# One down projection of a two-layer block: five of its eleven k-tile pairs by Strassen's 7-product form

## The reference, cut to what matters

```python
# first layer, x: (256, 1024)
x = x + (g_a * y_a + g_b * y_b) @ w_out           # mixer
h = rms_norm(x, ffn_norm_w)
gt, up = split(h @ w_gate_up, 2)                  # 2 x 2816 columns
x = x + (silu(gt) * up) @ w_down                  # w_down: (2816, 1024)   <- here
# second layer
h = rms_norm(x, norm1_g_2)
proj = h @ w_in_2                                 # next: x2, q, k, g2, v
...
x = x + square(relu(rms_norm(x, norm2_g_2) @ w_up_2)) @ w_down_2   # last projection
```

## Time and profile before

| | us |
|---|---|
| median of three runs | 717.55 |
| profiled execution, its own time | 717.69 |
| its span, first to last instruction | 716.0 |
| PE busy in the span | 710.5 |
| DVE busy | 535.0 |
| ACT busy | 424.2 |
| POOL busy | 190.6 |
| first down projection, first matmul to the first of `x2` | 378.89 to 440.11 |
| last down projection | about 630 to 712.7 |

### The profile page before, as it was taken

The page is one execution under the profiler, slowest core; times in us unless marked ns, Lnnn a source line. Parts: engine busy times, 40 slices in busy tenths (PEclk is TensorE's granted clock), DMA queues, the critical chain, the costliest instruction groups (busy, mean ns, idle before and its releaser), DMA issues.

```text
span 716.0 us, 9290 instructions
## 1 busy us (share of the span) xinstructions
PE 710.5 (99%) x3488; PEld 591.1 (83%) x3488; DVE 535.0 (75%) x715; ACT 424.2 (59%) x550; POOL 190.6 (27%) x128
## 2 busy tenths in 40 slices
PE   9999999999999999999999999999999999999998
PEld 7777878888888888888888888888889888888886
DVE  6899999999987665555556454678866577879997
ACT  7646676664893554444444255469845777865660
POOL 1298998989300030000000000144000134000000
PEclk9999999999999999999999999999999999999999
DMA  9877446455557556555665555633354565655541
GB/s 318 265 221 236 132 162 206 156 170 176 177 192 249 161 184 211 180 176 178 186 210 168 185 194 170 231 138 120 119 174 143 183 206 158 199 181 205 199 177 59
DMA packets 79739, 131.59 MB, mean 184 GB/s; under 512 B 4064, under 2 KB 37032, under 8 KB 79696
## 3 DMA queue, kind: packets, MB, share of 16 engines
q1 hardware_dynamic: 79008, 130.28, 55.0%
q10 hardware_dynamic: 544, 0.53, 0.2%
q0 software_dynamic: 144, 0.20, 0.1%
HBM read 129.75 MB, written 1.25 MB: 183 GB/s over the span
## 4 chain that ended last, share of the span: by engine, by line
PE 96%; DVE 1%; POOL 1%; DMA 1%; ACT 1%; issue 1%; SPq 0%; ACTq 0%
PE acc L1950 21%; PE acc L1952 21%; PE acc L1951 21%; PE aux L1906 4%; PE aux L1610 3%; PE acc L1906 3%; PE acc L1961 3%; PE acc L1962 3%; PE acc L1963 3%; PE aux L1912 2%; PE acc L1912 2%; PE aux L1962 1%; PE aux L1961 1%; PE aux L1963 1%; PE aux L1653 1%; PE aux L1671 1%
## 5 line engine op out<-in xcount | busy, mean ns | idle before, releaser
L1099 DVE TENSOR_TENSOR w_lo<-raw,w_hi 128x2048 fp32r<-128x2048 f32 (+1 forms) x96 | 215.2, 2246 | 86.3 <-ACT w_hi L745 86.3
L745 ACT ACTIVATE w_hi<-raw 128x2048 fp32r<-128x2048 f32 (+2 forms) x115 | 214.6, 1870 | 85.6 <-PE acc L1952 69.6
L1950 PE MATMUL acc<-w_hi,h_both 128*128 128x512 f32 x488 | 195.0, 400 | 0.4 <-DVE tok L1191 0.4
L1952 PE MATMUL acc<-w_hi,h_both 128*128 128x512 f32 x488 | 190.6, 391 | 0.0
L1951 PE MATMUL acc<-w_lo,h_both 128*128 128x512 f32 x488 | 190.1, 390 | 0.0
L1950 PEld LDWEIGHTS acc<-w_hi,h_both 128*128 128x128 f32 x488 | 91.7, 188 | 20.2 <-issue 1.4
L1952 PEld LDWEIGHTS acc<-w_hi,h_both 128*128 128x128 f32 x488 | 91.6, 188 | 19.7
L1951 PEld LDWEIGHTS acc<-w_lo,h_both 128*128 128x128 f32 x488 | 91.8, 188 | 17.7
L606 POOL TENSOR_TENSOR w_lo<-raw,w_hi 128x2048 fp32r<-128x2048 f32 x21 | 97.9, 4677 | 1.4 <-ACT w_hi L745 1.4
L1180 DVE SCALAR_TENSOR_TENSOR aux<-glu_t,vec_t,aux 128x256 f32<-128x256 f32 x232 | 93.6, 485 | 0.0
L629 POOL TENSOR_TENSOR rstd<-ms,nhalf 128x2 f32<-128x2 f32 x3 | 8.0, 2682 | 267.4 <-DVE ms L1161 256.5
(11 more groups left out here) (295 smaller groups left out, 1115.4 us busy)
## 6 DMA issues: line engine op xcount, KB each, us to landing
raw<-w_in_dram SPq DMA_DIRECT2D x29, 1024.0 KB, 5.2
raw<-w_down_dram SPq DMA_DIRECT2D x26, 1024.0 KB, 4.9
raw<-w_gate_up_dram SPq DMA_DIRECT2D x44, 512.0 KB, 4.8
raw<-w_up_dram SPq DMA_DIRECT2D x16, 1024.0 KB, 5.5
raw<-w_out_dram SPq DMA_DIRECT2D x8, 1024.0 KB, 5.1
raw<-w_in_dram SPq DMA_DIRECT2D x12, 512.0 KB, 4.7
raw<-w_proj_attn_dram SPq DMA_DIRECT2D x4, 1024.0 KB, 5.0
raw<-w_proj_conv_dram SPq DMA_DIRECT2D x4, 1024.0 KB, 5.0
```

The costliest lines, as they stand in the source:

```text
L745: ins = nc.scalar.activation(hi_cell(u)[:, part, :], src, ACT.Copy)
L1099: ins = nc.vector.tensor_tensor(lo_cell(u)[:, part, :], src, f(hi_cell(u)[:, part, :]), ALU.subtract)
L1950: nc.tensor.matmul(o, x_h, w_hi[:, slot, j, :], start=begin_, stop=False)
L1952: mm = nc.tensor.matmul(o, x_l, w_hi[:, slot, j, :], start=False, stop=end_)
```

## The change

The first down projection gets the same form as the last one.

- All 1024 columns are computed at once, pair of k-tiles by pair, in the order 0, 1, 2, 6, 3, 4, 7, 5, 8, 9, 10. Pairs 1 to 5 are fast (a `raw` and a `sum` unit), the other six are plain. That is 16 steps (62 to 77) in the place of 12, so B is 78 instead of 74.
- POOL makes the stationary sums of pairs 1 to 5 during the feed-forward stage. ACT first copies the turned tile to `ff_kept`, and later makes `m_hi` and `a_hi_f` from it; DVE makes `m_lo` and `a_lo_f`.
- DVE makes the weight sums of each fast pair (at step `s` those of unit `s + 4`).
- A fourth cell (`w_hi_3`, `w_lo_3`, where `h_both` lies) is used in this stage too, from step 64 to 75.
- The first pair (step 62) is multiplied for the right columns first; then PE waits for the last product of the feed-forward part (`ff_made` 22) and multiplies it for the left columns. Before the first fast product (step 63) PE claims all four `aux` banks, bank 0 with `ff_lo` 11, the last feed-forward pair read by DVE.
- DVE combines the seven products at step B-3 (step 75), the small chain moves from step 62 to step B-2 (76), and the left half is added to `x_res` at step B-1 (77).
- PE multiplies the last two pairs (steps 76, 77) by halves: both left halves, the right half of pair 9, then it waits for `added` 6, turns the left half of `x_res`, and multiplies the right half of pair 10.

```diff
+FAST_1, FAST_2 = range(1, 6), range(2, 10)
+GROUPS_1 = [0, 1, 2, 6, 3, 4, 7, 5, 8, 9, 10]
-    out += [("res", 2 + i, w["w_down"], CW * i, None, list(range(0, FK, UK)), FK) for i in range(2)]
+    out += [("res", 3, w["w_down"], 0, None, list(range(len(block_plan(GROUPS_1, FAST_1)))), KT * FK)]
...
+    for u in range(ALL):
+        wide = u in plan and u not in (D1, D1 + 1, B - 2, B - 1, NU, NU + 1, NU + 2)
+        cells = [k for k in range(SPLIT + 1) if k < SPLIT or wide]
+        if SPLIT in cells and users.get(SPLIT, 0) < (D1 if u < NU else NU):
+            users[SPLIT] = (D1 if u < NU else NU) - 1
+        cell = min(cells, key=lambda k: users.get(k, k - SPLIT))
+        cell_before.append(users.get(cell, -1))
...
@@ POOL
+                for i in FAST_1:
+                    if s == end["ff", i]:
+                        pool.wait_ge(ff_copied, FAST_1.index(i) + 1)
+                        stationary_sums(FAST_1.index(i), ff_kept[:, :].rearrange("p (a b) -> p a b", a=1),
+                                        a_sum[:, 0:1, :, :])
@@ ACT
-                    if s == end["ff", i] + 1:
+                    if s == end["ff", i] + 1 and i not in FAST_1:
                         pair_high(m_hi, i, i % 2, ff_turned, i + 1, ff_hi)
+                    if s == end["ff", i] + 1 and i in FAST_1:
...
+                        nc.scalar.activation(ff_kept[:, :], aux[:, i % 2, :], ACT.Copy).then_inc(ff_copied, 1)
...
+                if s == B - 1:
+                    square_of(2, 0)
+                    square_of(2, 1)
+                    stage_high(2, 0)
+                    stage_high(2, 1)
@@ DVE
+                if s < NU and s + LEAD + 2 in SUMS:
+                    weight_sums(s + LEAD + 2)
...
+                if s == B - 3:
+                    combine(True, None, None, (v_sum_1, w_sum_1, p_kept_1))
+                if s == B - 1:
+                    dve.wait_ge(combined, COMBINED)
+                    dve.wait_ge(last_block, 1)
+                    for t in range(NT):
+                        xr = x_res[:, t, 0:CW]
+                        nc.vector.tensor_tensor(xr, block_acc(s, 0, t), xr, ALU.add).then_inc(added, 1)
+                    stage_low(2, 0)
+                    stage_low(2, 1)
-                if s == begin["res", 2]:
+                if s == B - 2:
                     steps = [0]
@@ PE
+            def last_pairs():
+                for u in (B - 2, B - 1):
+                    wait_blocks(u)
+                tile_pair(B - 2, 0, False, False)
+                tile_pair(B - 1, 0, False, True).then_inc(last_block, 1)
+                tile_pair(B - 2, 1, False, False).then_inc(unit_done, 1)
+                pe.wait_ge(added, 6)
+                stage(2, (0, 1))
+                tile_pair(B - 1, 1, False, True).then_inc(unit_done, 1)
+            def blocks_unit(u):
+                kind, g = plan[u]
+                wait_blocks(u)
+                if u == D1:
+                    tile_pair(u, 1, True, False)
+                    pe.wait_ge(ff_made, 2 * FF // 256)
+                    mm = tile_pair(u, 0, True, False)
...
+                if kind == "raw":
+                    if is_first:
+                        if u < NU:
+                            claim(range(4), combined, COMBINED)
...
+                    product(aux[:, 0, :], u, 0, *of_m(2 * g, 0), is_first, is_last)
+                    product(block_acc(u, 0, 0), u, 1, *of_sum(u, g, 2), False, False)
+                    mm = product(block_acc(u, 1, 0), u, 2, *of_m(2 * g + 1, 0), False, False)
+                if kind == "sum":
+                    product(aux[:, 1, :], u, 0, *of_sum(u, g, 0), is_first, is_last)
+                    product(aux[:, 3, :], u, 1, *of_m(2 * g, 1), is_first, is_last)
+                    product(aux[:, 2, :], u, 2, *of_sum(u, g, 1), is_first, is_last)
+                    mm = product(block_acc(u, 1, 1), u, 3, *of_m(2 * g + 1, 1), False, False)
```

More of the change, by code:

```diff
@@ L55, with block_plan @@
 VROWS = 64
+FAST_1, FAST_2 = range(1, 6), range(2, 10)
+GROUPS_1 = [0, 1, 2, 6, 3, 4, 7, 5, 8, 9, 10]
+GROUPS_2 = [0, 1, 10, 2, 3, 11, 4, 5, 12, 6, 7, 13, 8, 9, 14, 15]
+def block_plan(groups, fast):
+    out = []
+    for g in groups:
+        out += [("raw", g), ("sum", g)] if g in fast else [("plain", g)]
+    return out
 def weight_chunks(w):
@@ L107, in build @@
     FAST_UPS = range(1, 5)
[L108 to L115, removed]
+    D1, B = begin["res", 3], begin["x2", 0]
+    plan = {D1 + p: x for p, x in enumerate(block_plan(GROUPS_1, FAST_1))}
+    plan |= {NU + p: x for p, x in enumerate(block_plan(GROUPS_2, FAST_2))}
+    ALL = max(plan) + 1
+    SUMS = [u for u in plan if plan[u][0] == "sum"]
+    LAST_FAST = {u < NU: u for u in SUMS}
+    raw_no, raw_user = [], []
+    for u in range(ALL):
+        if u not in SUMS:
+            raw_user.append(u)
+        raw_no.append(len(raw_user) - 1)
+    cell_of, cell_before, users = [], [], {}
+    for u in range(ALL):
+        wide = u in plan and u not in (D1, D1 + 1, B - 2, B - 1, NU, NU + 1, NU + 2)
[4 more added lines that the diff above has]
+        cell_before.append(users.get(cell, -1))
+        cell_of.append(cell)
+        users[cell] = u
+    LAST_WIDE = max(u for u in range(B) if cell_of[u] == SPLIT)
     PIECED = 3
@@ L120, in build @@
     raw_value = []
[L121 to L127, removed]
+    for r, u in enumerate(raw_user):
+        paired = u < NU and chunks[units[u][0]][4] is not None
+        raw_value.append((raw_value[r - RAW] if r >= RAW else 0) + (0 if u < PIECED else 32 if paired else 16))
     def on_pool(u):
@@ L558, in _ @@
                             sp.dma_start(tile[ps, :, ps], src).then_inc(lru_w_in, 16)
[L559 to L571, removed]
+            for u in range(NU, ALL):
+                if u not in SUMS:
+                    slot_free(u)
+                    pair_of_tiles(u, a["w_down_2"])
             o_rows = out.rearrange("b (t p) d -> p (b t) d", p=P)
@@ L1874, in after, with product, of_m @@
                     suffixes(3)
+            def product(o, u, j, a_h, a_l, begin_, end_):
+                w_h, w_l = hi_cell(u)[:, j, :], lo_cell(u)[:, j, :]
+                nc.tensor.matmul(o, a_h, w_h, start=begin_, stop=False, skip_group_check=True)
+                nc.tensor.matmul(o, a_h, w_l, start=False, stop=False, skip_group_check=True)
+                return nc.tensor.matmul(o, a_l, w_h, start=False, stop=end_, skip_group_check=True)
+            def of_m(kt, t):
+                return m_hi[:, kt, P * t:P * (t + 1)], m_lo[:, kt, P * t:P * (t + 1)]
@@ new lines, in tile_pair @@
+            def tile_pair(u, n, begin_, end_):
+                g = plan[u][1]
+                for k in range(2):
+                    for t in range(NT):
+                        mm = product(block_acc(u, n, t), u, 2 * k + n, *of_m(2 * g + k, t), begin_ and k == 0,
+                                     end_ and k == 1)
+                return mm
+            def last_pairs():
[7 more added lines that the diff above has]
+                tile_pair(B - 1, 1, False, True).then_inc(unit_done, 1)
@@ L1889, in _ @@
                     pe.wait_ge(*freed_by(c - 2))
+                if is_first and chunks[c][:2] == ("x2", 0):
+                    pe.wait_ge(added, 6)
+                if s in plan:
+                    if s == B - 1:
+                        last_pairs()
+                    elif s != B - 2:
+                        blocks_unit(s)
+                        after(s)
+                    continue
                 if is_first and chunks[c][:2] == ("up", 1):
```

359 lines of the change are left out of this document (205 added, 154 removed).

## The result

The changed kernel takes 721.97 us (median of four runs, 721.83 to 722.04) beside 717.8 us for the kernel before (717.4 to 718.11): 4.2 us slower, ratio 1.0058, 95% interval 1.0041 to 1.0076. The forecast was slower by 2.35 us, 719.9, with a range from 717.9 to 721.9.

A forecast was written before the change was run, and what follows sets the result against it. The prediction took PE's matmuls to bound the stage. Its terms, -3.4 + 1.7 + 0.65 + 3.4 = +2.35 us, on 717.55 us gave 719.9 us, with a range of 717.9 to 721.9 us.

The forecast's parts named there:

- PE's saving: First down projection: 249 matmuls in place of 264, 15 fewer at 0.227 us each, saving 3.4 us.
- The handover of bank 0: Step 62 to 63: PE must wait for DVE's low part of the last feed-forward pair, losing 1.7 us.
- The chain from unit 74 to the additions: Steps 74 to 78: DVE's list takes 17.0 us, PE asks after 13.6 us, so PE waits 3.4 us.
- POOL and ACT in the feed-forward stage: Feed-forward stage: the added sums and copies cost nothing, 0, at most 1 us.
- The end, from B on: From B on, each engine finds its list as before and the last down projection is unchanged: 0.
- The remark that moving the chain alone would leave a wait of 2 us in ACT's list: Step 77 on: without the small chain, ACT's late squares and copies would make PE wait 2 us.
- The term of 0.65 us for DVE's lag: Steps 63 to 75: PE waits briefly for DVE's low parts, 0.65 us, between 0 and 3.
- A rule that would add to this: Gap at B-1: an idle array falls back to 1.2 GHz; noted, but nothing added to the sum.
- rival 1: Behind the gap at B-1 the clock falls, adding 2.7 to 5.4 us: 722.6 to 725.3 us, chance 0.06.
- the prediction's own two signs of being wrong: Wait before the transposes under 1.5 us, or PE's clock below 1.00 anywhere behind it.
- Rivals 2 and 3: First: DVE bounds the whole stage, 721.4 to 723 us, chance 0.08. Second: DVE's list in time, 715.9 us, chance 0.09.
- Rival 3: Whole stage: DVE's list is in time, so only matmuls and handover count: 715.9 us, chance 0.09.

The follow-up runs named there:

- e2_chain: Changed kernel with only the chain of 15 small DVE operations moved from step B-2 to step B+1: 720.92 us.
- e4_bank: Changed kernel with only the last feed-forward pair turned into aux bank 2 in place of bank 0: 721.33 us.
- e6_lists_bank: e3_lists with only the last feed-forward pair put in aux bank 2, pairs in the old order: 716.81 us.
- e1_fill: Changed kernel with twelve unused matmuls of 512 columns put before PE's wait for the additions to x_res: 720.25 us.
- e3_lists: Changed kernel, small chain at B+1; at B-1 ACT squares and stages before copying unit 79, DVE adds to x_res before unit 78's low part: 717.22 us.
- e5_best: e3_lists with the last feed-forward pair in bank 2 and both middle plain pairs behind the second fast pair: 715.14 us.
- e8_lists_chain: e3_lists with the chain of 15 small operations back at step B-2, in front of the additions: 718.47 us.
- e10_fill6: Changed kernel with six unused matmuls in PE's gap at B-1, in place of the twelve of e1_fill: 720.29 us.

## Why the prediction was wrong

The direction, the place and the largest wait were right; the size was short by 1.8 us of 4.2, and the time lies 0.07 us outside the range. The fall of the clock is 1.7 us of this. Beside that the forecast started from 717.55 us, and the kernel before took 717.8 beside the changed one: by the change of 4.2 us alone, 721.7, the time would lie just inside the range.

**What held.** PE's saving, at the spacing of starts and not at the busy time of a row. The handover of bank 0 (1.7 forecast, 1.9 measured: DVE's low part ends at 386.45 us, and PE starts 0.31 us behind it, where 0.06 was reckoned). The chain from unit 74 to the additions: 17.0 us forecast; from 422.17, PE's first start behind unit 74, to 438.85 it took 16.7. PE asked after 13.6 us, as forecast, so the wait was 3.1 us and not 3.4. POOL and ACT in the feed-forward stage: 0, and POOL's sums took 0.46 us each, not 2.67. The end, from B on: 0. The remark that moving the chain alone would leave a wait of 2 us in ACT's list: 2.1 (e2_chain).

**What came out by luck.** The term of 0.65 us for DVE's lag. It was to be waits for DVE's low parts at pair 6 and pair 7. The trace has none of them: PE starts unit 67 at 396.60 us without a wait. That DVE is close behind is shown by e4_bank and e6_lists_bank, where PE comes earlier and waits until about 396.1 us for the low part of this unit. The 0.7 us measured are starts 0.2323 in place of 0.2267 us apart, a mechanism that the prediction doesn't have.

**What failed.** The sum, at the step "A rule that would add to this": it set the clock's price at 0 and left the fall to rival 1 at 0.06. The price was 1.7 us: the last 12 matmuls took 4.4 us in place of 2.7. A clock below 1.00 behind the wait was also one of the prediction's own two signs of being wrong. The fall came in all four runs (granted clock 0.997 or 0.998 of the whole kernel beside 0.999 or 1.0). The argument was that no row of before shows a fall, and that the gap is a single one; but before has no gap of this length (the longest wait of PE that its trace shows is 1.1 us), so its rows could say nothing against the rule. The forecast itself made one of 3.4 us. In this trace the granted clock is 0.50 from 440.5 to 443.2 us, and 1.00 with the gap filled (e1_fill). The rule of the Trainium skill, "TensorE: Matmul & The Clock Gate", section "Part 1: The HAM clock gate", that an idle array falls back to 1.2 GHz and works its way up again, agrees with both.

**The rival's size** was off the other way: 2.7 us for 12 matmuls at twice the spacing, 5.4 for more. Measured is 1.7. Behind the transposes the first two steps from start to start took 0.31 us, as at the restart at 386.76, and 0.35; then seven took 0.43, one 0.30, and the last two 0.24 and 0.23. (The Trainium skill, "TensorE: Matmul & The Clock Gate", section "Wait — 56ns, not 53.3ns?", gives 426.7 ns for cold matmuls of 512 columns; the trace agrees.)

**Rivals 2 and 3.** DVE was no bound of the whole stage, full as it is in the last projection: with its list in order the same passes fit (e3_lists, e5_best). Rival 3's case, all of DVE's list in time, is what e3_lists makes: 717.2, not 715.9. Its stage takes 60.4 us and not 61.2 - 3.4 + 1.7 = 59.5, by 0.2 us of the handover and 0.7 of slower starts; its profiled run is 0.3 us below its median.

**The chances.** Added up from the prediction's own parts, slower comes to 0.75 and same to 0.17, where it has 0.74 and 0.18. Nothing hangs on it.

## What to carry to other kernels

A form that spares PE matmuls for more passes elsewhere can lose it all again by the order of those passes: here the same operations gave 722.0 or about 715.3 us, by where three pieces stand in two lists, the bank of one pair and the order of the pairs. Before such a change, lay out what stands in each list between the last operand and what the busiest engine waits for, and take everything out of that stretch that is not needed there; then look for what is late next, since on the changed kernel the chain alone gave 1.05 us and the bank alone 0.6, and all moves together 6.4 to 6.8. Where the layout leaves TensorE standing still longer than it ever does in the trace before, price the lower clock as well: 1.7 us here, on top of a wait of 3.1.

## What the runs showed of the hardware that was not expected

- The clock fell after PE had gone back to work. PE stood still from 435.95 to 438.90 us; the granted clock was 1.00 through the eight transposes and until about 440.14, and the first steps of 0.43 us begin at 440.41. Who looks for the cause at the place of the slow matmuls finds a busy PE.
- The standstill and the fall, by kernel: 0.7 us (e8_lists_chain) and 1.6 us (e10_fill6), no run with a clock under 0.999; 2.1 us (e2_chain), three runs of five at 0.997; 3.0 us (changed kernel), four of four at 0.997 or 0.998. In e4_bank, with standstills of 1.5 and 2.9 us, one run of five shows none (1.0) and one shows 0.995, more than one fall as in the other traces gives; no trace of these two was kept.
- e2_chain, with its gap of 2.1 us, has two times on the same chip: 719.2 or 721.0 us. The median of five such runs says little.
- At a granted clock of 1.00 matmuls of one shape have two spacings: 0.2267 and 0.2323 us from start to start. The second stands in stretches of the first projection's fast pairs and a little beyond them, in every kernel above, and not in the same form's products of the last projection. What makes the difference is open.
